# Last two output tiles of a down projection in token halves, with an earlier weight split and a moved convolution schedule

## What is computed

```python
y = lax.conv_general_dilated(xpad, lp["conv_w"][:, None, :], window_strides=(1,), padding="VALID",
                             feature_group_count=C_CONV) + lp["conv_b"]      # 31 taps per channel
```

```python
h = rms_norm(x, lp["g_ffn_pre"])
gt, up = jnp.split(h @ lp["w_gate_up"], 2, axis=-1)
f = (jax.nn.silu(gt) * up) @ lp["w_down"]          # 2816 -> 1024
x = x + rms_norm(f, lp["g_ffn_post"])              # y_prompt, y_sample
```

## Time and profile before

| | us |
|---|---|
| median of 3 runs (lowest, highest) | 1208.33 (1208.24, 1209.09) |
| profiled execution, its time | 1207.61 |
| its span, first to last instruction | 1205.9 |
| TensorE busy | 1143.2 (95%) |
| VectorE busy | 569.2 (47%) |
| ScalarE busy | 435.9 (36%) |
| GpSimd busy | 382.6 (32%) |

### The profile page before, as it was taken

One profiled execution on the slowest core, in us unless ns is written; L12 is line 12 of the kernel. 1 busy time (PEld: TensorE's weight loads), 2 busy tenths in 40 slices (PEclk: granted clock), 3 DMA queues, 4 the chain that ended last, 5 costly groups with the idle time before them and its releaser, 6 DMA issues.

```text
span 1205.9 us, 25556 instructions
## 1 busy us (share of the span) xinstructions
PE 1143.2 (95%) x10914; PEld 1078.0 (89%) x10914; DVE 569.2 (47%) x987; ACT 435.9 (36%) x732; POOL 382.6 (32%) x192
## 2 busy tenths in 40 slices
PE   7999999999999987689899989999999999999994
PEld 7999899998999986479899957999999999999993
DVE  4567777667766445925546194362322223200005
ACT  4543432432423456322645343562232222222212
POOL 4331211220311233544622300332344433344442
PEclk9999999999999998899899999999999999999996
DMA  7321111120112422264614677321333323223311
GB/s 200 88 71 37 36 54 37 54 67 22 54 54 63 123 72 88 61 212 128 176 44 150 193 246 278 100 85 36 95 95 89 87 87 103 84 81 96 96 30 71
DMA packets 163465, 115.90 MB, mean 96 GB/s; under 512 B 5272, under 2 KB 153002, under 8 KB 163113
## 3 DMA queue, kind: packets, MB, share of 16 engines
q1 hardware_dynamic: 159835, 104.87, 29.1%
q10 hardware_dynamic: 3542, 9.75, 2.5%
HBM read 108.91 MB, written 6.17 MB: 95 GB/s over the span
## 4 chain that ended last, share of the span: by engine, by line
PE 46%; issue 35%; POOL 9%; DVE 6%; ACT 2%; DMA 1%; POOLq 0%; SPq 0%; DVEq 0%; ACTq 0%
PE ps L424 34%; PE ps L406 9%; POOL w_lo L734 9%; PE ps L845 2%; DVE cache L2472 1%; DVE sq_acc L2371 1%; DMA q_bc<-q_scratch 1%; DVE ps L2383 1%; DMA x_tok<-in_x_prompt_dram 0%; DVE x_res L2387 0%; DVE h_lo L2404 0%; DVE ps L2400 0%; DVE stat L2445 0%; ACT h_hi L1778 0%; DVE h_lo L2461 0%
## 5 line engine op out<-in xcount | busy, mean ns | idle before, releaser
L734 POOL TENSOR_TENSOR w_lo<-w_raw,w_hi 128x1024 fp32r<-128x1024 f32 (+1 forms) x141 | 327.4, 2323 | 646.1 <-ACT w_hi L459 646.1
L424 PE MATMUL ps<-h_hi,w_hi 128*128 128x260 f32 x1376 | 289.8, 292 | 8.1 <-DVE h_lo L2336 4.7
L424 PE MATMUL ps<-h_hi,w_lo 128*128 128x260 f32 x1376 | 277.9, 284 | 0.0
L424 PE MATMUL ps<-h_lo,w_hi 128*128 128x260 f32 x1376 | 277.5, 283 | 0.0
L424 PEld LDWEIGHTS ps<-h_hi,w_hi 128*128 128x128 f32 x1376 | 213.1, 189 | 19.4 <-POOL w_lo L734 7.9
L459 ACT ACTIVATE w_hi<-w_raw 128x1024 fp32r<-128x1024 f32 (+2 forms) x142 | 140.9, 993 | 207.1 <-PE ps L424 182.7
L424 PEld LDWEIGHTS ps<-h_hi,w_lo 128*128 128x128 f32 x1376 | 212.9, 189 | 0.0
L424 PEld LDWEIGHTS ps<-h_lo,w_hi 128*128 128x128 f32 x1376 | 212.6, 189 | 0.0
L2079 DVE SCALAR_TENSOR_TENSOR conv_y<-glu,prm,conv_y 128x512 f32<-128x512 f32 x120 | 102.6, 855 | 2.2
L845 PE MATMUL ps<-g,axb 64*64 64x128 f32 (+1 forms) x1024 | 78.0, 254 | 2.1 <-DVE g L2105 2.1
L2581 DVE TENSOR_TENSOR f_tmp<-ps,silu 128x520 f32<-128x520 f32 x19 | 13.3, 700 | 137.6 <-PE ps L424 137.6
(11 more groups left out here) (399 smaller groups left out, 2028.4 us busy)
## 6 DMA issues: line engine op xcount, KB each, us to landing
w_raw<-in_w_gate_up_dram SPq DMA_DIRECT2D x44, 512.0 KB, 3.9
w_raw<-in_w_in_dram SPq DMA_DIRECT2D x38, 512.0 KB, 4.0
cache<-in_cache_mem_k_dram SPq DMA_DIRECT2D x16, 512.0 KB, 6.6
cache<-in_cache_mem_v_dram SPq DMA_DIRECT2D x16, 512.0 KB, 6.1
w_raw<-in_w_down_dram SPq DMA_DIRECT2D x16, 512.0 KB, 4.0
w_raw<-in_w_k_dram SPq DMA_DIRECT2D x8, 512.0 KB, 4.0
w_raw<-in_w_v_dram SPq DMA_DIRECT2D x8, 512.0 KB, 3.7
w_raw<-in_w_out_dram SPq DMA_DIRECT2D x8, 512.0 KB, 3.9
```

The source lines that it names most:

```text
L424: mm = nc.tensor.matmul(ps[:, 2 * s + a, 0:width], w[:, k, :], x[:, x0 + k, a * width:(a + 1) * width], start=(first and k == 0 and n == 0 ...
L734: pool.tensor_tensor(lo[:, 0:kts], w_raw[:, b % RAW_SLOTS, 0:kts], hi[:, 0:kts].bitcast(F32), ALU.subtract).then_inc(w_lo_ready, 1)
```

## The change

1. **Down projection.** The loop runs three turns of six weight blocks (tiles 0 to 5). Tiles 6 and 7 are written out: both for the first token half (264 columns), then both for the second (256). `half_sum`, `half_root` and `half_add` of the first half come while TensorE works on the second half, and so do the turning, copying and storing of prompt tiles 0 and 1 and of the samples. In the second half the even blocks are scaled into a two-deep ring in PSUM and added by VectorE, the odd ones are scaled into `y_buf` and added by GpSimd. The rows are copied and stored in pieces of 512 columns (256 KB). `y_tok` now lies in the raw weight slots. ScalarE, not VectorE, copies y to `y_buf`. The table load stands ahead of the down projection.
2. **Weights.** Blocks 18 to 21 of the down projection (`B_LAST` on) have four high and four low slots of their own, where `h_hi` and `h_lo` lay. Blocks 18 to 21 are rounded before tile 5 is taken out of PSUM, blocks 22 and 23 behind it.
3. **Convolution.** `TAP_FILL` has no convolution steps behind updates 19, 20 and 21, and more behind 22 to 25: in the first pair 2, 2, 3, 2 in place of 1, 1, 2, 2 (and 1, 1, 2, 1 behind 26 to 29 as before), in the others 1, 2, 2, 2 in place of 1, 1, 1, 1.

```diff
-TAP_FILL = ((0,) * 6 + (2, 2, 2, 1, 2, 1) + (1,) * 12 + (2, 2, 1, 1, 2, 1), (0,) * 6 + (1,) * 22 + (0, 0))
+TAP_FILL = ((0,) * 6 + (2, 2, 2, 1, 2, 1) + (1,) * 7 + (0,) * 3 + (2, 2, 3, 2, 1, 1, 2, 1),
+            (0,) * 6 + (1,) * 13 + (0,) * 3 + (1, 2, 2, 2, 1, 1, 0, 0))
...
+        if B_LAST <= b < B_LAST + 4:
+            return wh_hi[:, b - B_LAST], wh_lo[:, b - B_LAST]
...
+        if B_LAST <= b < B_LAST + 4:
+            return B_DOWN
+        if b >= B_LAST + 4:
             return b - 5
...
+            for n, (j, d) in enumerate(((2, 0), (3, 0), (2, 1), (3, 1))):
+                if n < 3:
+                    sp.wait_ge(y_turn_a, 4 + n)
+                else:
+                    sp.wait_ge(y_turn_v, 3)
+                cols = slice(D // 2 * d, D // 2 * (d + 1))
+                sp.dma_start(y_prompt[0, P * j:P * j + P, cols], y_tok(j)[:, cols]).then_inc(stored, 16)
...
-            add_branch(p_ffn)
+            for k in range(1, KT, 2):
+                pool.wait_ge(odd_scaled, k // 2 + 1)
+                pool.tensor_tensor(x_res[:, k, TOK[2][1]], x_res[:, k, TOK[2][1]], y_buf[:, k, TOK[2][1]], ALU.add
+                                   ).then_inc(x_odd_ready, 1)
...
+            for m in range(KT - 2, KT):
+                for j in range(3):
+                    down_piece(m, j, 0)
+            down_piece(KT - 2, 0, 1)
+            half_sum(2, 0)
+            down_piece(KT - 2, 1, 1)
+            down_piece(KT - 2, 2, 1)
+            down_piece(KT - 1, 0, 1)
+            pe.wait_ge(a_taken, A_TAKEN + 2)
+            turn_tile(0, (0, 2), ready=KT * 4)
+            turn_tile(1, (4, 5))
+            down_piece(KT - 1, 1, 1)
+            pe.wait_ge(y_turn_a, 2)
             for k in range(KT):
...
+            down_piece(KT - 1, 2, 1)
+            half_sum(2, 1)
...
+            for m in range(KT - 2):
                 for j in range(3):
...
+                if m == KT - 3:
+                    for b in range(B_LAST + 1, B_LAST + 4):
+                        split_hi(b)
+                down_out(m, None)
+            for b in range(B_LAST + 4, N_BLOCKS):
+                split_hi(b)
+            down_out(KT - 2, 0)
+            down_out(KT - 1, 0)
+            half_root(4)
+            down_out(KT - 2, 1)
...
+            for k in range(0, KT, 2):
+                ring = ps[:, 4 + k // 2 % 2, 0:width]
+                if k >= 4:
+                    dve.wait_ge(post_x_ready, KT * 5 + k // 2 - 1)
+                scaled(k, ring).then_inc(branch_scaled, 1)
+                scaled(k + 1, y_buf[:, k + 1, cols]).then_inc(odd_scaled, 1)
+                dve.wait_ge(branch_scaled, KT * 5 + k // 2 + 1)
+                tt(x_res[:, k, cols], x_res[:, k, cols], ring, ALU.add).then_inc(post_x_ready, 1)
```

More of the change, by code:

```diff
@@ L515, in hybrid_step_kernel @@
     post_rsqrt, post_x_ready = sem("post_rsqrt"), sem("post_x_ready")
[L516 to L534, removed]
+    branch_scaled, x_odd_ready = sem("branch_scaled"), sem("x_odd_ready")
+    odd_scaled = sem("odd_scaled")
     a_done, a_taken, up_taken = sem("a_done"), sem("a_taken"), sem("up_taken")
@@ L1400, in _ @@
             pe.wait_ge(f_lo_ready, sum(DOWN_KT[:2]))
-            with pe.Fori(0, KT // 4) as i:
-                for u in range(12):
+            with pe.Fori(0, 3) as i:
+                for u in range(6):
                     b, o = B_DOWN + u, B_DOWN + u // 3
@@ L1417, in _, with down_piece @@
-            pe.wait_ge(y_turn_a, 1)
-            for k in range(KT):
-                mm = tr(ps[0:B, k // 4, P * (k % 4):P * (k % 4) + P], x_res[:, k, 0:B], ident[:, :])
-            mm.then_inc(y_turns, 1)
+                          last=(u % 3 == 2), taken=o // 2 + i if u % 3 == 0 else None, more=6 * i)
+            def down_piece(m, j, h):
+                b = B_DOWN + 3 * m + j
+                hi, lo = weights(b)
+                pe.wait_ge(w_lo_ready, b + 1)
+                if j == 0 and h == 0:
+                    pe.wait_ge(out_taken[m % 2], (B_DOWN + m) // 2)
+                k0 = sum(DOWN_KT[:j])
+                for k in range(DOWN_KT[j]):
+                    for n, (w, x) in enumerate(((hi, f_hi), (hi, f_lo), (lo, f_hi))):
+                        mm = nc.tensor.matmul(ps[:, 2 * (m % 2) + h, 0:TOK_N[2][h]], w[:, k, :], x[:, k0 + k, TOK[2][h]],
+                                              start=(j == 0 and k == 0 and n == 0),
+                                              stop=(j == 2 and k == DOWN_KT[2] - 1 and n == 2))
+                if j == 2:
+                    mm.then_inc(block_done if h else a_done, 1)
@@ new lines, in turn_tile @@
+            def turn_tile(j, banks, ready=None):
+                for k in range(KT):
+                    if ready is not None:
+                        pe.wait_ge(post_x_ready, ready + k + 1)
+                    mm = tr(ps[:, banks[k // 4], P * (k % 4):P * (k % 4) + P], x_res[:, k, B + P * j:B + P * j + P],
+                            ident[:, :])
+                mm.then_inc(y_turns, 1)
+            for m in range(KT - 2, KT):
+                for j in range(3):
+                    down_piece(m, j, 0)
```

152 lines of the change are left out of this document (85 added, 67 removed).

## The result

| | before | after |
|---|---|---|
| median of 4 runs on one chip (lowest, highest) | 1208.28 (1207.78, 1209.09) | 1199.27 (1196.51, 1201.16) |
| ratio, 95% interval | | 0.9923 (0.9899 to 0.9947) |
| profiled execution, its span | 1207.61, 1205.9 | 1196.51, 1194.8 |
| mean granted clock of the profiled execution | 0.978 | 0.985 |
| last dense matmul to the end of the span | 26.2 | 12.1 |

The forecast was 1199.2. The profiled execution was the fastest of the four, so its trace is 11.1 us shorter than that of before, while the medians differ by 9.0.

The account below looks back on a forecast made before the run. TensorE, never idle in the projections, and a 26.2 us tail behind it were taken to bound the kernel. Part 1's -9.9 and the convolution's +0.8 made -9.1: 1208.33 to 1199.2 us, range 1195.4 to 1202.6.

Parts of the forecast that it names:

- Part 1: Down projection's last two tiles in token halves: span from 1205.9 to about 1196.0 us, 9.9 less.
- the convolution edit: Mixer, three convolution steps moved behind updates 22 to 25: +0.8 us in sum, bounds -2.1 and +1.5.
- The dense part: Sum and transposes moved ahead of the last dense matmul cost full length: it ends 3.5 us later, at 1183.2.
- The tail: From last dense matmul to span end: falls from 26.2 to 12 or 13 us, ending at 1195.9.
- last store and end: Last 256 KB store: 0.5 us issue wait, 3.0 from issue to landing, 0.4 to the span's end.
- The arrival taken for the second pair, 211.6: Mixer: TensorE comes at about 211.6 now, 211.1 without the stall; second wg update done at 211.4.
- Rival A: Mixer: the convolution edit gains its full 2.1 us because VectorE catches up; 1196.3 us in all; chance 0.17.
- Rival B: Last additions: GpSimd and VectorE block each other, +3.0 us, 1202.2 in all; chance 0.13.
- Rival C: Output stores stay the limit: 2 KB rows at half rate add 0.65 to 2.6 us, 1201.8 at most; chance 0.06.
- Rival D: Down projection: earlier splits hold up ScalarE and a tile waits, up to +4 us, 1203.2; chance 0.04.
- Part 2: Splitting kept down-projection blocks one tile earlier, during tile 5: cost 0, covered by TensorE's dense work.
- Rival E: Second token half: waits drop TensorE's clock to half, 12.8 us more, 1212 in all; chance 0.03.

Follow-up runs that it names:

- all ten runs: The changed kernel's first four runs and six more on another chip; median 1198.26 us, the six alone at ratio 0.9923 to the kernel before.
- The version with the old schedule: Changed kernel with the convolution schedule put back, so parts 1 and 2 alone; 1197.5 us, ratio 0.9911 to the kernel before.
- 1.33 alone: Kernel before with only the new convolution schedule; 1209.64 us against 1208.51, ratio 1.0004; mixer +1.33 us in the trace.
- The spread schedule: Changed kernel with the three convolution steps moved ahead of GpSimd's split, none behind updates 20 and 21; 1194.15 us, ratio 0.9880; again 1193.07.
- the stores held back: Changed kernel with stores of prompt tiles 0 and 1 and samples issued only in the last stage; 1199.56 us, ratio 0.9931.
- The version with the late split: Changed kernel with ScalarE rounding weight blocks 19 to 21 behind the taking of tile 5, not before; 1200.27 us, ratio 0.9928.

## Why the prediction was right

The mechanism was right: the tail went and the work moved ahead of it cost its length. The hit to 0.1 us is luck. Part 1 gained 1.2 us more than forecast and the convolution edit cost 0.5 more, which leaves 0.7; and the median of these four runs, 1199.27, lies 1.0 us above that of all ten runs (1198.26). By its steps:

- **The dense part, +3.5.** Measured +3.0. Cover held everywhere: no wait in tiles 6 and 7. The transposes were priced too high: 16 took 1.75 and 8 took 0.87, not 1.95 and 0.98 as read off the busy time of 32 in an earlier stage; the first sum took 0.44 and not 0.57. The 0.2 us for changes of kind and the 0.2 us gained by narrower pieces were both about 0.
- **The tail, 12.7.** Measured 12.1. Term by term (forecast, measured): square and addition 0.9, 0.92; sum, root and start 1.55, 1.62; last odd product 4.25, 4.29; GpSimd's addition 0.75, 0.73; last transposes 0.7, 0.75; copy 0.65, 0.71; last store and end 3.9, 3.1. Only the last is off. Its issue followed after 0.3 and not 0.5, and the 256 KB landed in 2.33 us and not 3.0 (the first of the four stores took 2.04). The 3.0 was the median of loads in another stage, with other traffic beside them.
- **So parts 1 and 2** take off 11.1 us, and not 9.9 (the prediction's own terms, 1205.9 less 1195.9, make 10.0). The version with the old schedule measures 11.0 in medians.
- **The convolution edit, +0.8.** Measured +1.27 (1.33 alone, 1.37 undone). The direction was right, and in the first pair it was exact (+1.2). The other pairs were to give back 0.4 in all and gave about nothing (0.07 each in two, while the last lost 0.15). The 0.4 was the mis-sized term: it is the upper end of the 0.1 to 0.2 counted for two pairs, and it counts the last pair at 0. The waits for wg in these three pairs (1.5 us) are as long as the waits for g that went (1.5). The arrival taken for the second pair, 211.6, fits the trace of before, where that product starts at 211.54; but the rule given for it, the first pair's 126.02 moved by 85.8, would make 211.8.
- **Rival A**, the full 2.1 us: refuted. The stall was removed, but nine steps then stood behind updates 22 to 25, before wg, in place of six, and VectorE was late there. VectorE's idle time in the pairs 2 to 4, which spoke for it, lay ahead of the last updates and was used up by the three added steps. The spread schedule shows that the gain was to be had, and more.
- **Rival B**, 3.0 us of blocking: it did not come, for the reason given. With one input in PSUM neither engine was held up (0.41 and 0.73 us), and an earlier stage shows the same with GpSimd first (0.74 for two additions inside its 2.37 us). What the prediction did not see is that the price depends on the order: with both inputs in SBUF the same program would have lost 0.11 us a pair, not 0.75.
- **Rival C**, stores as the limit: did not come. Half of the output leaves early, which is worth 2.3 us. Rows of 2 KB do not move at half the rate: with the stores held back they went out at 400 GB/s (1194.0 to 1195.5 us), against 406 for those of 4 KB before.
- **Rival D**, ScalarE held up: the late load came (3.57 us) and was covered. Part 2 was priced at nothing as an edit, rightly; but it carries 1.7 us of part 1, which the prediction did not say.
- **Rival E**, half clock in the second half: from 1167.3 to 1182.7 us, where TensorE is busy 15.38 of 15.40 us, the granted clock reads 1.00. Without a wait there was nothing to bring it about. The version with the late split has one, of 1.7 us in the first half tile, and its clock reads 1.00 from 1150 to 1185.4 us all the same; two waits, as the rival had them, were not tried.

The forecast put -9.1 on the whole; by the traces' own terms it is -11.1 + 1.3 = -9.8, and the runs say -10.0 (1208.28 less the 1198.26 of all ten) or -10.3 (1208.51 less 1198.26, on one chip). Why some executions of this kernel take 5 to 7 us more than others was not seen stretch by stretch, since the two that were profiled, 1195.76 and 1196.51, are among its three shortest.

## What to carry to other kernels

A last stage that cannot overlap with anything shrinks when the last tiles are computed in halves: everything per column is done early for one half, at the price of what moves into the dense stream, which here was 3 us for 14. When a stall of an in-order engine is removed by moving work behind it, count that work again up to the next place where someone waits for this engine; here the stall of 0.56 us came back as two, of 1.06 and 0.69. When VectorE's and GpSimd's operations both read only SBUF and overlap, see which of them starts first: here that decided between 0.11 and 1.0 us for one addition. Work that TensorE must do but that need not be done before its last dense product belongs into its wait for the final statistics, not ahead of them.

## What the runs showed of the hardware

- Of an addition of VectorE and an operation of GpSimd that overlap and read only SBUF, the one that starts later pays the rest of the other, less about 0.15 us: 0.11 us for GpSimd when VectorE started 0.16 us ahead (0.84 in place of 0.73, and 0.42 for VectorE), 1.0 us for VectorE when GpSimd's had 1.10 us left (1.66 in place of 0.69 at 520 columns), and 1.2 when it had 1.35 left (1.64 in place of 0.42 at 264).
- VectorE's additions with one input in PSUM kept their time beside GpSimd, whoever was first: 0.41 us at 1186.03 (VectorE first), and 0.74 for two at 780.60 (GpSimd first, from 779.84 to 782.21).
- SyncE's issues of stores grow longer when many follow one another: 0.36, 0.42, 0.72 us, and the four behind them 3.15 together, against 0.36 for one by itself and 0.33 to 0.43 for each of the last four in the kernel after.
- A store of 256 KB landed 2.04 us after its issue with no other under way when it was issued, 2.33 us when issued 0.37 us behind another in the same queue, and 2.7 us when issued 0.09 us behind one in a second queue.
- Executions of one kernel on one chip lay up to 7.0 us apart (1195.76 to 1202.79 in six runs, with mean granted clocks of 0.986 to 0.981), and 1.3 us in the four of the spread kernel.
- Stores in rows of 2 KB moved at 400 GB/s, those in rows of 4 KB at 406.
